# Gates of a gated linear attention computed beside the Fourier products of the same mixer

## The chip, the core and the metric

The kernel is one program on one core of a Trainium2 chip. The metric is the device time of one execution in microseconds (us). The five engines are named as in the profile: PE (TensorE, the matrix products; PEld is its weight load), DVE (VectorE), ACT (ScalarE), POOL (GpSimd) and SP (SyncE, which here only issues transfers).

## What is computed

The reference runs two transformer blocks of two layers each, one after the other. The stage that matters here is the mixer of the first layer of the second block, on 256 context and 512 latent tokens (768 in all). Its input projection gives a part for a Fourier mix, the queries, keys, values and output gate of a gated linear attention (GLA), and a 16-wide `z` from which the decay gates of both directions are made:

```python
def fourier_mix(u):
    ug = u.reshape(B_, L, FOURIER_GROUPS, FOURIER_GROUP_DIM).astype(jnp.float32)
    f = jnp.fft.fft2(ug, axes=(1, 3), norm='ortho').real
    ...
def even_mix(h, s_f, s_b, w_in, w_gate, b_gate, g_gla, w_out):
    p = h @ w_in
    u_f, q, k, v, r, z = jnp.split(p, EVEN_SPLITS, axis=-1)
    loga = [heads(jax.nn.log_sigmoid(zf @ w_gate[d] + b_gate[d]) / GLA_GATE_TEMP, GLA_DK) for d in range(2)]
    o_f, s_f = gla_scan(q, k, v, loga[0], s_f)
    o_b, s_b = gla_scan(flip(q), flip(k), flip(v), flip(loga[1]), s_b)
    ...
    y = jnp.concatenate([fourier_mix(u_f), o], axis=-1) @ w_out
```

`gla_scan` walks over chunks of tokens. Inside a chunk the scores are q·k weighted with the exponential of a difference of the running sums of `loga`, and a state is carried from chunk to chunk. Everything is in float32.

## The kernel before

Activations lie with features on the 128 partitions and tokens along the free axis. Large products run over weight tiles of 128 columns, which SP fetches, ACT and DVE split into a high and a low part (lines 282 and 290), and PE multiplies (lines 312 and 338). Each engine has its own program written out by hand (`pe_program`, `act_program`, `dve_program`, `pool_program`, `sp_program`). An instruction waits only for the semaphores that it names (`seen`), and an engine runs its instructions strictly in the order of its program. So the order of the work around the change is the order of calls in these five functions.

Four stages follow each other in this mixer:

- **Input product** (`pe_in2`, `act_in2`). 17 tiles. Tiles 0 to 8 go to `z2` (keys, queries, output gate, `z`), 9 to 16 to `more` (values in 0 to 3, Fourier input in 4 to 7). At its end PE turns the four value tiles (line 583) into PSUM banks 4 and 5, and ACT copies each out to `v2` (line 592).
- **Fourier** (`pe_fourier`, `act_fourier`, `dve_fourier`). Four groups. For each, PE multiplies with the feature basis `dft_f` into banks 4 to 6 (line 1760), ACT copies the rows to `more[:, 0:2]` (line 1779), and PE multiplies these with the token bases `dft_ctx` and `dft_lat` into banks 4 and 5 (line 1768). ACT copies them out (lines 1783 and 1784) and rounds them to `h_hi` (line 1786), and DVE makes `h_lo` (line 520). One set of buffers serves all groups, so each step waits for the one before.
- **Gates** (`pe_gl_gates`, `act_gl_gates`, `dve_gl_gates`), once per direction: a product with 16 rows (line 1839), copies out with the bias (1849), minus the absolute value on DVE (1863), exponential (1853), a table load (1855), logarithm (1856), then on DVE the log-sigmoid (1865), the running sum with a reset at each chunk (1871), and for the second direction a reversal (1879 and 1881).
- **Scores** (`pe_gla`, `act_gla`, `dve_gla`). Score 0 is the diagonal. Then come 14 steps, 7 levels for each direction. In a step DVE makes the arguments of the decay (lines 634 and 635), ACT the exponential (641), DVE multiplies it with q and k (650), PE makes the products (734) and DVE copies those under a mask into `gatt` (760). Scores 0, 1, 2, 8 and 9 are wide (24 products of 128 columns in three groups), the other ten are narrow (48 rows of the trace, products of 64 columns, in two groups). DVE makes the arguments one step ahead. After these come the state products and the normalization, and then the output product.

The gates of direction 0 are made ahead of score 0, and those of direction 1 between scores 2 and 3. The masks come as 640 KB of int32 into the space of `gatt`. POOL widens them into uint8 masks in 15 casts (line 698) and zeroes `gatt` after that (line 1831). The first masked copy waits for the zeroing.

What runs on both sides of the changed stretch is the product of `in2` on PE and the last products of the scores:

```python
    for i in range(steps):
        c = gl_combs(k)[i % 3]
        pe.wait_ge(*k.seen("decayed", ("g", i)))
        pe_scores(k, "g", i + 1, c, c, GL_UNITS, GL_STEPS)
```

## Time and profile before

| what | us |
|---|---|
| three runs, median (lowest to highest) | 2997.51 (2995.91 to 3006.83) |
| the profiled execution, its own time | 2994.43 |
| its span in the profile | 2993.1 |
| PE, DVE and ACT busy in the span | 2644.7, 1786.8 and 1079.9 |
| window 1441 to 1508 (turning, Fourier): PE busy | 50.45 of 67 |
| window 1508 to 1527 (gates of direction 0): PE and DVE busy | 3.71 and 9.54 of 19 |
| window 1527 to 1554 (scores 0 to 2): PE and DVE busy | 18.18 and 24.00 of 27 |
| window 1554 to 1574 (gates of direction 1): PE and DVE busy | 9.91 and 9.38 of 20 |
| window 1574 to 1640 (scores 3 to 14): PE and DVE busy | 55.23 and 60.48 of 66 |

All times in the trace count from the start of the span. The timeline merges neighbouring instructions of one kind: start, duration, engine, line, operation, tiles, count, and in brackets how long the engine had been idle and who ended that. The chain of waits is the sequence of work that ended last, followed back from the end: what stands in it set the end, and what doesn't was covered. PEclk is the granted clock of PE as a share of 2.4 GHz: 1.00 is that level, 0.50 is 1.2 GHz, and values between are means over a window in which both occurred.

### The profile page before, as it was taken

The page shows a single profiled execution, that of the slowest core. Times are in us where ns is not written, and L with a number is a line of the kernel's source. Part 1 is how long each engine was busy: PE and PEld are TensorE (multiplying, and loading weights), DVE is VectorE, ACT ScalarE, POOL GpSimd, SP SyncE. Part 2 cuts the span into 40 slices and gives each one's busy share as a digit, 9 for nine tenths or more (in the row PEclk, how much of TensorE's full clock was granted, in tenths as well). Part 3 has the DMA queues.
Part 4 walks back from the last instruction along what each step waited for, and adds up shares of the span by engine and source line. Part 5 has one row for each costly group of instructions (what it writes and reads, how often), then busy time and mean ns, then how long its engine had stood idle before and what let it go on. Part 6 is the DMA issues. An engine that isn't in the chain of part 4 may idle for free.

```text
span 2993.1 us, 32376 instructions
## 1 busy us (share of the span) xinstructions
PE 2644.7 (88%) x13240; PEld 2200.5 (74%) x13240; DVE 1786.8 (60%) x2436; ACT 1079.9 (36%) x1413; POOL 32.7 (1%) x48
## 2 busy tenths in 40 slices
PE   5946589999939999989857899999999888899999
PEld 4846377888827888868537778888888766678887
DVE  6574668888688877741059455524553577465464
ACT  3242244323245325342233453312332555343342
...
DMA packets 80275, 295.06 MB, mean 99 GB/s; under 512 B 8944, under 2 KB 11632, under 8 KB 79872
## 3 DMA queue, kind: packets, MB, share of 16 engines
...
## 4 chain that ended last, share of the span: by engine, by line
PE 79%; DVE 13%; ACT 5%; issue 2%; DMA 0%; POOL 0%; DVEq 0%; ACTq 0%
PE ps L312 66%; PE ps L338 3%; PE ps L734 2%; PE ps L2326 1%; PE ps L1768 1%; PE ps L2294 1%; DVE gatt L760 1%; DVE h_lo L520 1%; DVE w_lo L290 1%; DVE p_lo L2596 1%; DVE anm L2578 1%; PE ps L1005 1%; DVE x L1344 1%; ACT h_hi L514 0%; DVE x L1357 0%
## 5 line engine op out<-in xcount | busy, mean ns | idle before, releaser
L312 PE MATMUL ps<-h_hi,w_hi 128*128 128x512 f32 (+1 forms) x2416 | 811.8, 371 | 64.5 <-DVE w_lo L290 38.0
L312 PE MATMUL ps<-h_lo,w_hi 128*128 128x512 f32 (+1 forms) x2416 | 805.0, 368 | 0.0
L312 PE MATMUL ps<-h_hi,w_lo 128*128 128x512 f32 (+1 forms) x2416 | 804.9, 368 | 0.0
L290 DVE TENSOR_TENSOR w_lo<-w_raw,w_hi 128x1024 fp32r<-128x1024 f32 (+2 forms) x323 | 414.7, 1284 | 573.8 <-ACT w_hi L282 573.1
L282 ACT ACTIVATE w_hi<-w_raw 128x1024 fp32r<-128x1024 f32 (+2 forms) x323 | 357.5, 1107 | 876.8 <-PE ps L312 843.4
L312 PEld LDWEIGHTS ps<-h_hi,w_hi 128*128 128x128 f32 x2416 | 456.5, 189 | 150.2 <-DVE w_lo L290 42.2
L312 PEld LDWEIGHTS ps<-h_hi,w_lo 128*128 128x128 f32 x2416 | 456.2, 189 | 77.6
L312 PEld LDWEIGHTS ps<-h_lo,w_hi 128*128 128x128 f32 x2416 | 456.6, 189 | 76.4 <-issue 2.2
L312 PE MATMUL ps<-g_hi,w_hi 128*128 128x512 f32 (+1 forms) x880 | 295.7, 369 | 0.8 <-DVE w_lo L290 0.8
L312 PE MATMUL ps<-g_lo,w_hi 128*128 128x512 f32 (+1 forms) x880 | 294.8, 368 | 0.0
L312 PE MATMUL ps<-g_hi,w_lo 128*128 128x512 f32 (+1 forms) x880 | 294.8, 368 | 0.0
L434 DVE CUSTOM_DVE_ANT_0 m_raw<-m_raw,c_act,small 128x1024 f32<-128x1024 f32 x179 | 226.4, 1280 | 1.6 <-DMA m_raw<-in_ada_w 1.6
L359 DVE SCALAR_TENSOR_TENSOR x<-ps,mods,x 128x512 f32<-128x512 f32 (+1 forms) x112 | 75.3, 690 | 198.0 <-PE ps L312 190.2
L312 PEld LDWEIGHTS ps<-g_hi,w_hi 128*128 128x128 f32 x880 | 165.3, 188 | 29.6 <-DVE w_lo L290 1.4
L312 PEld LDWEIGHTS ps<-g_lo,w_hi 128*128 128x128 f32 x880 | 165.3, 188 | 28.2 <-issue 0.5
L312 PEld LDWEIGHTS ps<-g_hi,w_lo 128*128 128x128 f32 x880 | 165.3, 188 | 27.8
L1487 DVE SCALAR_TENSOR_TENSOR conv_u<-ps,small,conv_u 128x510 f32<-128x510 f32 (+2 forms) x220 | 148.6, 692 | 3.1
L1443 ACT ACTIVATE g_hi<-gated 128x512 fp32r<-128x512 f32 (+1 forms) x88 | 60.4, 686 | 223.8 <-DVE gated L1500 223.8
L1438 ACT ACTIVATE silu_u<-conv_u 128x512 f32<-128x512 f32 (+1 forms) x88 | 60.4, 687 | 191.9 <-DVE conv_u L1487 191.9
L338 PE MATMUL ps<-h_hi,w_hi 128*128 128x256 f32 (+1 forms) x192 | 66.0, 399 | 60.9 <-DVE w_lo L290 35.2
L1502 DVE TENSOR_TENSOR g_lo<-gated,g_hi 128x512 fp32r<-128x512 f32 (+1 forms) x88 | 66.8, 759 | 66.2 <-ACT g_hi L1443 66.2
L338 PEld LDWEIGHTS ps<-h_hi,w_hi 128*128 128x128 f32 x192 | 37.6, 203 | 77.2 <-issue 52.7
...
## 6 DMA issues: line engine op xcount, KB each, us to landing
...
```

Source lines behind the costliest of these rows:

```text
L282: act.activation(k.w_hi[s][:, 0:w], k.w_raw[s][:, 0:w], ACT.Copy).then_inc(*k.tick("w_hi", g))
L290: dve.tensor_tensor(k.w_lo[s][:, 0:w], k.w_raw[s][:, 0:w], k.w_hi[s][:, 0:w].bitcast(F32), ALU.subtract).then_inc(*k.tick("w_lo", g))
L312: last = pe.matmul(ps[:, bank, 0:tn], a[:, c, :], b[:, c, t0:t0 + tn], start=c == 0 and n == 0, stop=c == kt - 1 and n == 2)
L338: last = pe.matmul(ps[:, bank, 0:tn], a, b[:, c, t0:t0 + tn], start=c == 0 and n == 0, stop=c == KD - 1 and n == 2)
L359: last = dve.scalar_tensor_tensor(x, k.ps[:, 2 * s + bank, 0:tn], gates[bank], x, ALU.mult, ALU.add)
L434: dve.tensor_tensor_reduce(w, w, k.c_act[:, last, :], 1.0, bias, ALU.mult, ALU.add, column(last)).then_inc(*k.tick("mods", job.key))
L520: k.nc.vector.tensor_tensor(k.h_lo[:, f, ts], value, k.h_hi[:, f, ts].bitcast(F32), ALU.subtract).then_inc(*k.tick("h_lo", key))
L734: last = pe.matmul(out, lhs[rows, cols], right, start=True, stop=True)
L1438: act.activation(f["silu"][:, :], f["conv"][0][:, :], ACT.Silu).then_inc(*k.tick("silu", g))
L1443: act.activation(f["hi"][:, j, :], f["g"][:, :], ACT.Copy).then_inc(*k.tick("g_hi", (block, layer, half, j)))
L1487: last = dve.scalar_tensor_tensor(o, ps[:, bank, lo - d:hi - d], w, o, ALU.mult, ALU.add)
L1502: dve.tensor_tensor(f["lo"][:, j, :], f["g"][:, :], f["hi"][:, j, :].bitcast(F32), ALU.subtract).then_inc(*k.tick("g_lo", key))
```

## The change

Gates of both directions move into the Fourier stage. The Fourier stage itself gets a second set of row buffers and of PSUM banks (0 to 3 by turns for the token products, 4 to 6 for the features), and its feature products run one group ahead. The turning of the values alternates between two pairs of banks. The running sums go to the upper half of `h_hi`, the log gates to the upper half of `h_lo` (both are free once the input product is done), the reset pattern and the chunk ends to places of their own. The reset pattern is loaded before the input product's later tiles. The masks now land in the space of `gkdt0`, so that POOL zeroes `gatt` first; each cast signals by itself, and each masked copy waits for its own mask. The same signals replace the single one in the HGRN stage of the first block.

```diff
+        self.gtop = Place(nc, sb.at + 4 * 4 * TALL)("gtop", [P, 4 * TALL])
...
+        self.greset = fo("greset", [P, TALL])[:, :]
+        self.gends = fo("gends", [P, 2, 12])
...
-        self.gb = [gl(f"gb{d}", [P, 2 * TALL]) for d in range(2)]
+        self.gb = [self.gtop[:, d * 2 * TALL:(d + 1) * 2 * TALL] for d in range(2)]
...
@@ pool_masks
+        pool.tensor_copy(mask_of(masks, steps, i).rearrange("p (u c) -> p u c", c=n), part.unsqueeze(1).to_broadcast([P, 1 if n == P else 4 * directions, n])
+                         ).then_inc(*k.tick("mask_" + label, i))
@@ dve_scores
+    dve.wait_ge(*k.seen("mask_" + label, i))
@@ sp_in2
+    sp.dma_start(k.greset, k.ins["reset2"]).then_inc(*k.tick("load", "reset2", 16))
@@ pe_fourier
+    pe_gl_gates(k, 0)
+    pe_fo_values(k)
+    pe_fo_features(k, 0)
+    pe_gl_gates(k, 1)
+    for g in range(4):
+        if g + 1 < 4:
+            pe_fo_features(k, g + 1)
+        pe_fo_time(k, g)
...
+def pe_fo_features(k, g):
+    pe = k.nc.tensor
+    if g == 0:
+        pe.wait_ge(*k.seen("load", "dft"))
+        pe.wait_ge(*k.seen("turned_out", ("v2", 3)))
+    else:
+        pe.wait_ge(*k.seen("fourier_rows", g - 1))
...
+def pe_fo_time(k, g):
+    pe, a = k.nc.tensor, fo_rows(k, g)
+    pe.wait_ge(*k.seen("fourier_rows", g))
+    pe.wait_ge(*(k.seen("fourier_out", g - 2) if g >= 2 else k.seen("gl_biased", 1)))
...
+def act_fourier(k):
+    act_gl_biased(k, 0)
+    for f in range(4):
...
+        act.activation(k.v2[:, :, f * P:(f + 1) * P], got, ACT.Copy).then_inc(*k.tick("turned_out", ("v2", f)))
+    act_fo_rows(k, 0)
+    act_gl_biased(k, 1)
+    for d in range(2):
+        act_gl_exp(k, d)
+    act_fo_rows(k, 1)
+    for d in range(2):
+        act_gl_log(k, d)
     for g in range(4):
+        act_fo_out(k, g)
+        if g + 2 < 4:
+            act_fo_rows(k, g + 2)
...
+def dve_fourier(k):
+    dve, q = k.nc.vector, gl_views(k)[0]
+    dve.tensor_scalar(q, q, 0.125, None, ALU.mult).then_inc(*k.tick("gl_q"))
+    for d in range(2):
+        dve_gl_abs(k, d)
+    for d in range(2):
+        dve_gl_gates(k, d)
     for g in range(4):
-        dve_low(k, "fourier", g, slice(0, TALL), k.more[:, 2, :])
+        dve_low(k, "fourier", g, slice(0, TALL), k.rstd[:, :])
@@ sp_gla
-    sp.wait_ge(*k.seen("h_lo", ("fourier", 3)))
-    sp.dma_start(k.greset, k.ins["reset2"]).then_inc(*k.tick("load", "reset2", 16))
     sp.wait_ge(*k.seen("load", "reset2"))
-    sp.dma_start(mask_stage(k.gatt, 2), k.ins["masks2"]).then_inc(*k.tick("load", "masks2", 16))
+    sp.wait_ge(*k.seen("fourier_t", 3))
+    sp.dma_start(mask_stage(k.gkdt[0], 2), k.ins["masks2"]).then_inc(*k.tick("load", "masks2", 16))
@@ pool_gla
+    pool.wait_ge(*k.seen("fourier_t", 3))
+    pool.memset(k.gatt[:, :, :], 0.0).then_inc(*k.tick("zeroed", "g"))
     pool.wait_ge(*k.seen("load", "masks2"))
-    pool_masks(k, "g", k.gmasks, k.gatt, 2)
-    pool.wait_ge(*k.seen("masks", "g"))
-    pool.memset(k.gatt[:, :, :], 0.0).then_inc(*k.tick("zeroed", "g"))
+    pool_masks(k, "g", k.gmasks, k.gkdt[0], 2)
@@ pe_gla
-    pe.wait_ge(*k.seen("h_lo", ("fourier", 3)))
-    pe_gl_gates(k, 0)
     pe.wait_ge(*k.seen("gl_k2"))
...
-        if i + 1 == 2:
-            pe.wait_ge(*k.seen("kept", BASE["in2"] + 16))
-            pe_gl_gates(k, 1)
-            pe.wait_ge(*k.seen("gl_biased", 1))
@@ act_gla
-    act_gl_gates(k, 0)
     for i in range(len(GL_STEPS)):
         act_decay(k, "g", i, gl_combs(k)[i % 3], s16)
-        if i == 2:
-            act_gl_gates(k, 1)
@@ dve_gla
-    dve.tensor_scalar(q, q, 0.125, None, ALU.mult).then_inc(*k.tick("gl_q"))
-    dve_gl_gates(k, 0)
+    dve.wait_ge(*k.seen("fourier_t", 3))
     dve.tensor_scalar(comb, kk, 2.0, None, ALU.mult).then_inc(*k.tick("gl_k2"))
...
-        if i == 2:
-            dve_gl_gates(k, 1)
```

PE in the Fourier stage, from the feature product of group 0 on. Of before (1760 are features, 1768 token products):

```order
L1760 MATMUL ps<-dft_f,z2more 128x256 [waits turned_out,load]
L1760 MATMUL ps<-dft_f,z2more 128x256 x5
L1768 MATMUL ps<-dft_ctx,z2more 128x256 [waits fourier_rows]
L1768 MATMUL ps<-dft_ctx,z2more 128x256 x3
L1768 MATMUL ps<-dft_lat,z2more 128x512 x8
L1760 MATMUL ps<-dft_f,z2more 128x256 [waits fourier_out]
L1760 MATMUL ps<-dft_f,z2more 128x256 x5
L1768 MATMUL ps<-dft_ctx,z2more 128x256 [waits fourier_rows]
L1768 MATMUL ps<-dft_ctx,z2more 128x256 x3
```

Of the change (1785 features, 1906 gates, 1798 token products):

```order
L1785 MATMUL ps<-dft_f,z2more 128x256 [waits turned_out,load]
L1785 MATMUL ps<-dft_f,z2more 128x256 x5
L1906 MATMUL ps<-z_143,tmp_68 128x256 [waits gl_biased]
L1906 MATMUL ps<-z_143,tmp_68 128x512
L1906 MATMUL ps<-z_143,tmp_68 128x256
L1906 MATMUL ps<-z_143,tmp_68 128x512
L1785 MATMUL ps<-dft_f,z2more 128x256 [waits fourier_rows]
L1785 MATMUL ps<-dft_f,z2more 128x256 x5
L1798 MATMUL ps<-dft_ctx,z2more 128x256 [waits gl_biased,fourier_rows]
L1798 MATMUL ps<-dft_ctx,z2more 128x256 x3
L1798 MATMUL ps<-dft_lat,z2more 128x512 x8
```

The gate products of direction 1 and the features of group 1 now stand ahead of the token products of group 0, and no feature product waits for `fourier_out` any more.

DVE from the end of the Fourier stage to the first arguments of the decay. Of before (520 is `h_lo` of the four groups, 2088 the doubled keys that score 0 needs):

```order
L520 TENSOR_TENSOR h_lo<-z2more,h_hi 128x768 [waits h_hi] x4
L2086 TENSOR_SCALAR z_142<-z_142 128x1536
L1863 SCALAR_TENSOR_TENSOR gb_147<-gcomb 128x1536 [waits gl_biased]
L1865 SCALAR_TENSOR_TENSOR gcomb<-gcomb,gb_147 128x1536 [waits gl_log]
L1871 SCALAR_TENSOR_TENSOR gb_147<-spare,gcomb 128x768 [waits load,gl_loga]
L1871 SCALAR_TENSOR_TENSOR gb_147<-spare,gcomb 128x768
L1875 COPY gends<-gb_147 128x12 [waits gl_b]
L2088 TENSOR_SCALAR gcomb<-z_142 128x1536
L634 TENSOR_TENSOR gkdt_152<-gb_147 128x768 [waits gl_q]
L635 TENSOR_TENSOR gkdt_152<-gb_147 128x768
L634 TENSOR_TENSOR spare<-gb_147 128x384x2
```

Of the change (1842 scales q, 1937 to 1958 are the gates of both directions, 521 is `h_lo`):

```order
L1842 TENSOR_SCALAR z_143<-z_143 128x1536
L1937 SCALAR_TENSOR_TENSOR gtop<-spare 128x1536 [waits gl_biased] x2
L1944 SCALAR_TENSOR_TENSOR spare<-spare,gtop 128x1536 [waits gl_log]
L1950 SCALAR_TENSOR_TENSOR gtop<-greset,spare 128x768 [waits load,gl_loga]
L1950 SCALAR_TENSOR_TENSOR gtop<-greset,spare 128x768
L1954 COPY gends<-gtop 128x12 [waits gl_b]
L1944 SCALAR_TENSOR_TENSOR spare<-spare,gtop 128x1536 [waits gl_log]
L1950 SCALAR_TENSOR_TENSOR gtop<-greset,spare 128x768 [waits gl_loga]
L1950 SCALAR_TENSOR_TENSOR gtop<-greset,spare 128x768
L1956 TENSOR_TENSOR gtop<-gtop,spare 128x1536 [waits gl_b]
L1958 TENSOR_TENSOR gends<-gtop,spare 128x12 [waits gl_back]
L521 TENSOR_TENSOR h_lo<-rstd,h_hi 128x768 [waits h_hi] x4
```

The whole gate work stands ahead of the four `h_lo` operations, and the doubled keys follow straight behind these.

DVE between the masked copies of score 2 and those of score 3. Of before:

```order
L760 COPY_PREDICATED gatt<-gmasks,ps 128x2x512 [waits scored] x2
L1863 SCALAR_TENSOR_TENSOR gb_148<-gkdt_151 128x1536 [waits gl_biased]
L1865 SCALAR_TENSOR_TENSOR gkdt_151<-gkdt_151,gb_148 128x1536 [waits gl_log]
L1871 SCALAR_TENSOR_TENSOR gb_148<-spare,gkdt_151 128x768 [waits gl_loga]
L1871 SCALAR_TENSOR_TENSOR gb_148<-spare,gkdt_151 128x768
L1879 TENSOR_TENSOR gb_148<-gb_148,gkdt_151 128x1536 [waits gl_b]
L1881 TENSOR_TENSOR gends<-gb_148,gkdt_151 128x12 [waits gl_back]
L634 TENSOR_TENSOR spare<-gb_147 128x48x16 [waits scored,gl_back]
L635 TENSOR_TENSOR spare<-gb_147 128x48x16
L650 TENSOR_TENSOR gkdt_152<-gkdt_152,z_142 128x96x8 [waits decay]
L650 TENSOR_TENSOR gkdt_152<-gkdt_152,z_142 128x96x8
```

Of the change:

```order
L762 COPY_PREDICATED gatt<-gmasks,ps 128x2x512 [waits scored] x2
L635 TENSOR_TENSOR spare<-gtop 128x48x16 [waits scored]
L636 TENSOR_TENSOR spare<-gtop 128x48x16
L651 TENSOR_TENSOR gkdt_153<-gkdt_153,z_143 128x96x8 [waits decay]
L651 TENSOR_TENSOR gkdt_153<-gkdt_153,z_143 128x96x8
L762 COPY_PREDICATED gatt<-gmasks,ps 128x128x4 [waits scored,att,mask_g]
```

The six operations of the second direction's gates are gone from between them, and the masked copy has one more name among its waits.

## Rows read from the trace of the kernel before

**Rows 1.** Page: shares of the chain that ended last, by engine.
```profile
PE 79%; DVE 13%; ACT 5%; issue 2%; DMA 0%; POOL 0%; DVEq 0%; ACTq 0%
```

**Rows 2.** Chain of waits, Fourier stage: start us, us, engine, tile, line.
```profile
1442.16 0.89 PE ps L583 x6
...
1448.58 0.82 ACT v L592
1449.53 2.84 PE ps L1760 x12
...
1463.72 2.87 PE ps L1760 x12
...
1468.12 8.87 PE ps L1768 x24
...
1477.94 2.87 PE ps L1760 x12
```

**Rows 3.** Chain of waits, from the last Fourier product to the first scores.
```profile
1499.84 5.59 PE ps L1768 x13
...
1507.23 0.97 DVE h_lo L520
...
1508.34 3.72 PE ps L1839 x8
...
1512.08 2.00 ACT gcomb L1849 x4
...
1526.65 0.86 DVE gcomb L2088
```

**Rows 4.** Timeline of DVE around the gates of the second direction.
```profile
1553.16 1.29 DVE L760 COPY_PREDICATED gatt<-gmasks,ps 128x1024 f32<-128x1024 uint8 x1 [1.01 <-PE ps L734]
...
1573.94 0.96 DVE L634 TENSOR_TENSOR spare<-gb 128x768 f32<-128x768 f32 x1
...
1575.68 1.82 DVE L650 TENSOR_TENSOR gkdt<-gkdt,z 128x768 f32<-128x768 f32 x2
1577.42 1.83 DVE L760 COPY_PREDICATED gatt<-gmasks,ps 128x512 f32<-128x512 uint8 x2
```

**Rows 5.** Timeline of PE: Fourier products, gate products, groups of scores.
```profile
1455.73 7.03 PE L1768 MATMUL ps<-dft_lat,z2more 128*128 128x512 f32 x16
...
1553.04 5.48 PE L1839 MATMUL ps<-z,tmp 16*128 16x256 f32 x8
...
1604.87 2.08 PE L734 MATMUL ps<-spare 64*128 64x128 f32 x16 [0.77 <-DVE gatt L760]
...
1612.98 1.16 PE L734 MATMUL ps<-gcomb 64*128 64x128 f32 x16 [0.77 <-DVE gatt L760]
1613.98 2.79 PE L734 MATMUL ps<-gkdt 64*128 64x64 f32 x48
```

**Rows 6.** Chain of waits, the last three steps of scores.
```profile
1624.20 15.73 PE ps L734 x144
```

**Rows 7.** Timeline of POOL, and two operations of DVE beside it.
```profile
1516.49 12.78 POOL L698 CAST gmasks<-gatt 128x128 uint8<-128x128 int32 x15 [657.12 <-DMA gatt<-in_masks]
1529.32 2.66 POOL L1831 MEMSET gatt<- 128x3072 f32 x1
...
1528.71 1.36 DVE L635 TENSOR_TENSOR gkdt<-gb 128x768 f32<-128x768 f32 x1
1529.99 0.95 DVE L634 TENSOR_TENSOR spare<-gb 128x768 f32<-128x768 f32 x1
```

**Rows 8.** Windows of 5 us: busy us of PE, PEld, DVE, ACT, POOL, then PEclk.
```profile
1505.00:1510.00 5.00, 2.08 (x7) 1.11 (x7) 1.83 (x2) 1.71 (x3) 0.00 (x0) 1.00 0.16 34
1510.00:1515.00 5.00, 2.05 (x4) 0.43 (x2) 0.89 (x1) 1.99 (x4) 0.00 (x0) 0.51 0.35 111
...
1590.00:1595.00 5.00, 5.00 (x50) 5.00 (x48) 5.00 (x7) 1.48 (x1) 0.00 (x0) 0.50 0.01 3
```

**Rows 9.** DMA issues: KB each, us from issue to landing.
```profile
gatt<-in_masks SPq DMA_DIRECT2D x1, 640.0 KB, 3.8
```

122 lines of the change are left out of this document (63 added, 59 removed).

## The prediction

> **What bounds the kernel now.** I read the views from the outside in. The page's chain by engine says that PE's products end 79% of the span [rows 1], so anything off PE pays only where PE stands still. The windows by stage (the table above) show where that is: in the gates of direction 0 PE works 3.7 us of 19, in those of direction 1 9.9 of 20. The chain of waits then tells what ends each stretch. In the Fourier stage it alternates between PE and ACT: features 2.87 us, the copy of the rows, token products 8.87 us, the copy out, and from one group's features to the next's 1477.94 - 1463.72 = 14.22 us [rows 2]. PE works 11.74 of these and waits 2.48. Behind the last token product the chain runs through one engine after another, none busy beside the other: `h_lo`, the gate products, the biased copies, then on to the doubled keys [rows 3]. The same happens for direction 1 between scores 2 and 3 [rows 4]. From score 3 on DVE and PE are both full, and the last three steps belong to PE [rows 6].
>
> **The change, part by part.** Times are on the clock of the old trace, where the last product tile has been copied at 1442.1.
>
> *1. The Fourier stage.* PE now makes the gate products of direction 0 first. Their 4 products are 2 of 256 and 2 of 512 columns; a 512-column product is two rows of 7.03/16 = 0.44 us [rows 5], so at that clock 4 x 0.44 + 4 x 0.22 = 2.7 us, to about 1444.9. Measured nearby are 3.72 (where the clock falls in the middle, [rows 3]) and 5.48 us at half clock [rows 5], which are the upper bounds; I take 2.7, since PE comes from a dense product at full clock. ACT's biased copies take 2.00 us [rows 3], then four copies of turned values at 0.82 [rows 2]: 1444.9 + 2.0 + 3.3 and some handing over, 1450.9. PE turns tiles 2 and 3 in that time. Features 0 start there, 1.4 us later than before [rows 2], and the values' two pairs of banks save what the gates would otherwise have cost. Then PE does 4 features (2.87 each), the second gate products (2.7) and 4 token products (8.87 each): 49.7 us, to about 1500.5, against 1499.84 + 5.59 = 1505.4 before [rows 3]. **Gain 4.9 us.** Nothing of it waits, if ACT keeps up: rows 0 end at 1455.5, the biased copies of direction 1 at 1458.5, and the token products of group 0 start at 1459.3; this is the tightest place, with 0.8 us. The two exponentials, rows 1, the table load and the two logarithms are done by about 1467.8, when those products end at 1468.2. DVE's gate work follows at 1466: two log-sigmoids of 1.8, four sums of 1.7 to 2.0, a reversal of 1.8, in all to about 1479.5. The copy out of group 1 waits for `h_lo` of group 0 behind that, about 1480.5, and PE needs that buffer and rows 3 only at 1491, 7 us later. So the gates cost nothing on the path but their two products.
>
> *2. From the last token product to score 0.* Before: from 1505.4 to the doubled keys at 1526.65 [rows 3], 21.2 us. Now: copies out, `h_hi`, `h_lo`, which end at 1508.20 [rows 3], 2.8 us after the products, and the doubled keys follow at once, since they stand behind `h_lo` of group 3 on DVE's queue. **Gain 18.4 us.** Beside it stand POOL's zeroing (2.66 us [rows 7], done at 1503.2) and the masks: 3.8 us from issue to landing [rows 9], 1504.3, and the first cast is a short one. The first masked copy comes at about 1511. None of the two is late, and the casts, 12.8 us for 15 [rows 7], keep ahead of steps of 5 to 8 us. ACT's table load stands behind the last `h_hi` and ends before the first argument does.
>
> *3. Between scores 2 and 3.* Before: from 1553.16 + 1.29 = 1554.45 to the arguments at 1573.94, 19.5 us [rows 4]; all of it goes. What is late next is PE: the 48 products of score 3 may start only when score 2 has been copied, and take 15.73/3 = 5.24 us at half clock [rows 6]. DVE needs 1577.42 - 1573.94 = 3.5 us to the masked copies and 0.9 for their first half, so the second half waits 0.9 us or a little more. From there both engines go at 5.2 us a step and the lag stays. **Gain 19.5 - 1.1 = 18.4 us.**
>
> *4. POOL beside DVE.* The casts used to run beside the sums and the first arguments, now beside the first two pairs of arguments, the first products with q and k and the first masked copies. The trace shows one operation at 1.36 us beside the casts and its like at 0.95 without [rows 7]. Four operations of DVE more than before are exposed: 4 x 0.41 = 1.7 us. Bounds: 0 if the casts slip between, 4 us if the three masked copies and the second step's operations suffer as well. **Loss 1.7 us.** The Trainium skill (GPSIMD Engine Reference, 1. Specifications) says that POOL shares its SBUF interfaces with VectorE and contends with instructions that have two SBUF inputs; a masked copy here reads its data from PSUM, so by that rule it stays clear and the loss ends at these 1.7 us. The row on the arguments agrees with it.
>
> *5. The rest.* The 384 KB of the reset pattern now queue behind the Fourier bases, ahead of a weight tile. I count nothing for it; the tile is due one whole product after its issue. 15 masked copies in this stage wait for one signal more; a copy with two satisfied waits starts while its predecessor ends (1575.68 + 1.82 = 1577.50 against 1577.42 [rows 4]), so I count 0, and at most 0.1 us each, 1.5 us. The HGRN stage keeps its order: 0.
>
> **Sum.** 4.9 + 18.4 + 18.4 - 1.7 = 40.0 us off the profiled execution's 2994.43, which gives 2954.4. The runs shown have their median 3.1 us above that execution; against it the forecast is 2997.5 - 40 = **2957.5 us**.
>
> **The rivals.**
>
> *The clock stays up.* After the Fourier stage the granted clock was 1.00, then 0.51 as PE did the 16-row gate products and stopped [rows 8]. This gap shrinks to 3.7 us, and the one between scores 2 and 3 vanishes. If PE kept 2.4 GHz through the scores, a wide group would take 1.16 in place of 2.08 us and a narrow score 2.79 in place of 5.24 [rows 5, 6]: five wide scores save 0.9 each, the lag of 1.1 us goes, and the end, where PE alone is the chain, becomes bound by DVE, about 4.5 us less. In all 10 us, 2947 us. Against it: from 1590 to 1595 PE was busy 5.00 of 5.00 us and its clock was 0.50 [rows 8], so being busy with these half-height products did not raise it. The Trainium skill (TensorE: Matmul & The Clock Gate, What's actually happening) has it that activity of PE releases the throttled clock; taken as PE's busy time, that speaks for this rival, and the row speaks against it. Chance 8%.
>
> *The Fourier stage doesn't close up.* ACT's queue is now long, and strictly in order: if a logarithm or a biased copy is late, token products wait as before. At worst all four gaps of 2.48 us stay, and PE still has 5.4 us of gate products more: the gain of 4.9 turns into a loss of 5. Result 2967 us. The slack of 0.8 us in part 1 speaks for a part of it, the 7 us behind it against more. Chance 10%.
>
> *The gates cool the clock, and the change loses.* The two gate products use 16 of 128 rows, and the clock fell during such products at 1510 [rows 8]. If they now pull the clock down at 1443 and again at 1454, and it doesn't come back, the 47 us of features and token products take twice the time: 47 + 5 us more against a gain of 40, so 3009 us, 0.4% slower than before; it decides from 40 us of PE's work at half clock. Against it: the old stage turned values with PE idle half of the time and kept 1.00. And the full-height products come in blocks of over 8 us, after which I expect it back. A short dip costs 3 to 5 us, and is in the range. Chance 2%.
>
> *The waits are there anyway.* Something I take as covered (landing of the masks, zeroing, a table load) takes the place of the gates' chain in part 2. The most that could stand there is the masks' landing and all 15 casts, which would hold the masked copy of score 0 to 1517, 6 us late: 2963 us. The casts signal one by one, so this means that the change doesn't do what it says. Chance 4%.
>
> **How the numbers follow.** The forecast with its small terms has 76%, the rivals 8, 10, 2 and 4%. The likeliest case with its bounds (casts 0 to 4 us, waits up to 1.5, a dip of the clock up to 5, and some us that a median of runs moves) goes from 2950 to 2966. The range reaches to the clock rival and to the Fourier rival: **2945 to 2968**. A measurement of this kernel can tell about 0.5%, 15 us, from no change. Faster by more than that: all cases but the slower one and mishaps of over 25 us that I can't name, 95%; within: 4%; slower by more: 1%.
>
> **What would show it.** In the changed profile: the token products of the groups with no idle time of PE between groups; the last one ending near 1500.5; the doubled keys about 2.8 us behind; POOL's casts from about 1504; no idle stretch of DVE between scores 2 and 3 but about 1 us; the clock at 0.5 in the scores again. The forecast is wrong if PE waits at the token products, if the clock stands below 1.00 after 1450, or if the masked copy of score 0 waits for a mask.

## The result, and the profile after

The change took **2956.47 us** (median of 4 runs, 2951.5 to 2959.81) beside 2996.71 us before (median of 4): a ratio of 0.9861, with a 95% interval from 0.9829 to 0.9894, or 40.2 us less. The forecast was 2957.5 us, in a range of 2945 to 2968. The profiled execution of the change took 2959.81 us, its span is 2958.5.

To see where the time went, the trace is cut at four points that every kernel here has: the first product behind the input product's last tile (start), the end of the last token product, the first masked copy, and the end of the last one. Behind these the work runs on to the first product of the output projection, which closes the **stretch**.

| | before | after | forecast |
|---|---|---|---|
| start to end of the last token product | 63.26 | 59.55 | 58.3 |
| from there to the doubled keys | 21.14 | 2.69 | 2.8 |
| from there to the first masked copy | 28.05 | 9.88 | |
| first to last masked copy | 107.77 | 88.12 | |
| last masked copy to the output projection | 37.79 | 37.97 | |
| the stretch (sum without the second row) | 236.87 | 195.52 | 196.9 |
| ahead of the start | 1442.2 | 1434.8 | |
| behind the stretch | 1314.1 | 1328.2 | |

The stretch is 41.3 us shorter, the forecast 40.0. Outside it the change only moves the loading of the reset pattern and splits the masks' signal in the first block, and there the one execution is 7 us shorter ahead and 14 longer behind. That is told under the control run below; it is the reason why the stretch, and not the span, is compared from here on.

One execution of `control` took 4478.48 us at a mean granted clock of 0.554, and the ratios below leave it out.

The page's chain now has PE at 80% (79% before, [rows 1]) and DVE at 12%:

```profile
PE 80%; DVE 12%; ACT 4%; issue 2%; DMA 0%; POOL 0%; DVEq 0%; ACTq 0%
```

The timeline of PE in the Fourier stage answers to [rows 2]. 1906 is the gate products, 1772 the turning, 1785 features, 1798 token products; the bracket is the idle time before:

```profile
1434.83 3.32 PE L1906 MATMUL ps<-z,tmp 16*128 16x256 f32 x8 [1.05 <-ACT z2more L351]
1438.08 5.68 PE L1772 MATMUL ps<-ident,z2more 128*128 128x128 f32 x24
1444.75 2.83 PE L1785 MATMUL ps<-dft_f,z2more 128*128 128x256 f32 x12 [0.99 <-ACT v L1809]
1447.51 2.84 PE L1906 MATMUL ps<-z,tmp 16*128 16x256 f32 x8
1450.28 4.54 PE L1785 MATMUL ps<-dft_f,z2more 128*128 128x256 f32 x12
...
1463.26 2.75 PE L1785 MATMUL ps<-dft_f,z2more 128*128 128x256 f32 x12
...
1474.44 2.75 PE L1785 MATMUL ps<-dft_f,z2more 128*128 128x256 f32 x12
```

Behind 1444.75 no row of this view has a bracket until the last token product ends: PE never waits again in this stage. A group takes 1474.44 - 1463.26 = 11.18 us, where it took 14.22. One row stands out: the features of group 1 took 4.54 us, their likes 2.75. The windows (busy us of PE, PEld, DVE, ACT, POOL, then PEclk) show what went with it. Up to the last token product three windows have a granted clock below 1.00, and each holds gate products or what stands right behind them:

```profile
1435.00:1440.00 5.00, 5.00 (x17) 3.13 (x17) 0.00 (x0) 1.81 (x4) 0.00 (x0) 0.70 0.01 3
1440.00:1445.00 5.00, 3.97 (x18) 3.20 (x17) 1.76 (x1) 3.31 (x5) 0.00 (x0) 0.62 0.00 0
...
1450.00:1455.00 5.00, 5.00 (x15) 3.88 (x15) 1.76 (x1) 4.16 (x6) 0.00 (x0) 0.66 0.00 0
```

The gate work on DVE, in its timeline, ends at 1472.20 + 0.18, and `h_lo` of group 0 follows:

```profile
1472.20 0.18 DVE L1958 TENSOR_TENSOR gends<-gtop,spare 128x12 f32<-128x12 f32 x1
1472.30 0.95 DVE L521 TENSOR_TENSOR h_lo<-rstd,h_hi 128x768 fp32r<-128x768 f32 x1
```

The chain of waits behind the last token product answers to [rows 3]. The gate products, the biased copies and the logarithm are gone from it:

```profile
1477.19 17.20 PE ps L1798 x48
...
1496.19 0.96 DVE h_lo L521
1497.15 0.87 DVE gcomb L2153
```

DVE goes on from there to score 3 nearly without a break; the timeline near the start and at the end of that answers to [rows 4]. 635 and 636 are the arguments, 651 the decayed products, 762 the masked copies:

```profile
1498.81 1.04 DVE L636 TENSOR_TENSOR gkdt<-gtop 128x768 f32<-128x768 f32 x1
...
1501.70 2.64 DVE L651 TENSOR_TENSOR gkdt<-gkdt,z 128x768 f32<-128x768 f32 x2
1504.26 2.48 DVE L762 COPY_PREDICATED gatt<-gmasks,ps 128x1024 f32<-128x1024 uint8 x2
...
1523.18 1.29 DVE L762 COPY_PREDICATED gatt<-gmasks,ps 128x1024 f32<-128x1024 uint8 x1 [1.00 <-PE ps L735]
1524.37 0.94 DVE L635 TENSOR_TENSOR spare<-gtop 128x768 f32<-128x768 f32 x1
...
1530.04 1.25 DVE L762 COPY_PREDICATED gatt<-gmasks,ps 128x1024 f32<-128x1024 uint8 x1 [1.51 <-PE ps L735]
```

The arguments follow the copies of score 2 at once (1524.37), where 19.5 us lay between them. What is late next is PE, as its own timeline (the row that answers to [rows 5] and [rows 6]) shows: 5.38 us for the 48 products of score 3, at a granted clock of 0.50 (window 1525 to 1530), and DVE's last row above waits 1.51 us for them.

```profile
1524.62 5.38 PE L735 MATMUL ps<-gcomb 64*128 64x64 f32 x48 [1.48 <-DVE gatt L762]
```

POOL zeroes first and casts behind it (compare [rows 7]); the masks land ahead of the first cast:

```profile
1494.44 2.66 POOL L1885 MEMSET gatt<- 128x3072 f32 x1 [639.58 <-PE ps L1798]
1498.33 10.86 POOL L699 CAST gmasks<-gkdt 128x128 uint8<-128x128 int32 x15 [1.24 <-DMA gkdt<-in_masks]
```

The narrow scores keep their clock of [rows 8], 0.50 with PE busy 5.00 of 5.00 us. In windows with wide scores it is above 0.50 at times, as it was before.

```profile
1530.00:1535.00 5.00, 5.00 (x51) 5.00 (x50) 4.96 (x6) 1.48 (x1) 0.00 (x0) 0.50 0.01 3
```

### The profile page after: what moved, and what is told of

It is laid out like the page before. It is cut to its first block, busy times and chain, and to the rows that moved or that the text cites. A ratio compares the mean times of both kernels' runs of the same rounds, so it can differ in the third digit from the quotient of the medians.

```text
span 2958.5 us, 32375 instructions
## 1 busy us (share of the span) xinstructions
PE 2654.1 (90%) x13240; PEld 2208.0 (75%) x13240; DVE 1786.1 (60%) x2436; ACT 1076.8 (36%) x1411; POOL 30.7 (1%) x48
## 4 chain that ended last, share of the span: by engine, by line
PE 80%; DVE 12%; ACT 4%; issue 2%; DMA 0%; POOL 0%; DVEq 0%; ACTq 0%
PE ps L313 67%; PE ps L339 3%; PE ps L735 2%; PE ps L2389 1%; PE ps L1798 1%; PE ps L2357 1%; DVE gatt L762 1%; DVE h_lo L521 1%; DVE w_lo L291 1%; DVE p_lo L2659 1%; DVE anm L2641 1%; DVE x L1346 1%; DVE x L1359 0%; ACT h_hi L515 0%; PE ps L1007 0%
```

## The experiments

Eleven further runs were made, in three groups, each with the kernel before on the same chip. The stretch and its parts, from one profiled execution of each:

| kernel | Fourier | to the first masked copy | masked copies | rest | stretch | ratio to before [95%] |
|---|---|---|---|---|---|---|
| before | 63.26 | 28.05 | 107.77 | 37.79 | 236.87 | |
| the change | 59.55 | 9.88 | 88.12 | 37.97 | 195.52 | 0.9861 [0.9829, 0.9894] |
| control | 56.44 | 9.88 | 88.10 | 38.17 | 192.59 | 0.9859 [0.9812, 0.9906] |
| again | 56.48 | 9.88 | 88.09 | 38.20 | 192.65 | 0.9846 [0.9823, 0.9868] |
| gates0_back | 53.97 | 27.63 | 87.72 | 40.01 | 209.33 | 0.9916 [0.9882, 0.995] |
| gates1_back | 55.32 | 9.88 | 106.93 | 37.93 | 210.06 | 0.9904 [0.9877, 0.9931] |
| serial_fourier | 69.40 | 9.88 | 88.10 | 38.25 | 205.63 | 0.9889 [0.9859, 0.9919] |
| masks_once | 56.61 | 17.56 | 88.84 | 39.63 | 202.64 | 0.9893 [0.9876, 0.9909] |
| early_masks | 59.56 | 8.78 | 89.16 | 37.98 | 195.48 | 0.9864 [0.9849, 0.9879] |
| tall_gates | 55.72 | 9.88 | 88.12 | 39.60 | 193.32 | 0.9868 [0.9842, 0.9894] |
| filler | 56.43 | 9.89 | 110.53 | 39.81 | 216.66 | 0.9931 [0.9916, 0.9947] |
| early0 | 59.48 | 1.78 | 88.83 | 38.89 | 188.98 | 0.982 [0.9796, 0.9844] |
| early0_tall | 55.72 | 1.79 | 89.72 | 37.64 | 184.87 | 0.9808 [0.9785, 0.9832] |

The last part (the column "rest") moves by itself by up to 2.4 us. In `gates0_back`, `masks_once`, `tall_gates`, `filler` and `early0` the last four products before the output projection took 2.66 to 2.90 us, in the other traces 1.53, and all but the last of these five also took longer over the first products with `v`. The work there is the same in all, and `tall_gates`, whose edit is far ahead of it, has 39.60 us where `control` has 38.17.

### The change itself, twice more

Neither has an edit.

> The changed kernel once more, to see what moves between two executions of one program. My theory: the stretch from the end of the input product to the first product of the output projection is fixed by its queues and repeats to 1 us (194.6 us in the trace of the change, 236.9 in that of before), and what the total moved less than that (34.6 us between the two spans, not 42.3) belongs to the other stages: dense weight products there take 8.32 us a tile in some stretches and 8.48 in others, the same in both kernels but in other places. Rival: the change itself puts the slower pace into the feed-forward stage behind it; then this run shows 8.48 us there again, and 8.32 in the input product.

> The change once more, unchanged, beside the two kernels below on one chip. The times outside the changed stretch differed by some 14 us between the profiled executions so far, with ACT's split of a 1024-row weight tile coming every 8.32 us in some stretches and every 8.48 in others. Theory (this is a property of the execution and not of the kernel): a median within 2952 to 2962 us and a stretch of 192.6 to 195.5 us, and some stretches of weight products at 8.32 and some at 8.48 us again. Rival (the first profiled run of the change was the odd one): all stretches at 8.32 us and a span near 2947 us.

Measured: stretches of 192.59 and 192.65 us, so 44.2 us below before; the first trace of the change, at 195.52, had 3 us more, all of it in the Fourier stage. So the theory of `control` that the stretch repeats to 1 us fails, between the first trace and the two repeats. (Its 194.6 us for that trace end one block of products early, at 1629.38; to the landmark of the table it is 195.52.) The median of `again` was 2953.49 us beside 2996.21. In the parts outside the stretch, the first trace of the change has 1328.2 us behind it, control 1317.2. Where these differ can be seen on ACT, which splits a weight tile of 1024 rows each time PE has finished one. In the input product, two stretches of the same work, of before and of the change, each at a granted clock of 1.00. Before:

```profile
1356.50 1.06 ACT L282 ACTIVATE w_hi<-w_raw 128x1024 fp32r<-128x1024 f32 x1 [6.66 <-PE ps L312]
...
1364.98 1.06 ACT L282 ACTIVATE w_hi<-w_raw 128x1024 fp32r<-128x1024 f32 x1 [6.66 <-PE ps L312]
```

The change:

```profile
1359.00 1.06 ACT L283 ACTIVATE w_hi<-w_raw 128x1024 fp32r<-128x1024 f32 x1 [6.50 <-PE ps L313]
...
1367.32 1.06 ACT L283 ACTIVATE w_hi<-w_raw 128x1024 fp32r<-128x1024 f32 x1 [6.50 <-PE ps L313]
```

A tile comes every 8.48 us in the one and every 8.32 in the other. Both paces occur in both kernels: behind the stretch, before goes at 8.32 and the first trace of the change, from 1738 on, at 8.48, and `control` and `again` go at 8.48 ahead and 8.32 behind. Of the twelve traces with the change or a part of it, four (the first one, gates0_back, serial_fourier, tall_gates) go at 8.48 over most of what lies behind the stretch and take 1327 to 1329 us there, the other eight go at 8.32 and take 1317 to 1318. Ahead of it, the six traces with 8.48 start the stretch at 1437.6 to 1443.4, and before, which goes at 8.48 there too, at 1442.2: the work on the first block and the moved loading show no price. So it is the theory of `again` that holds: 11 of the 14 us behind the stretch belong to the execution and not to the change. The other 3 are in all twelve traces, against one trace of before; aligned with it, those of control arise in the attention, 650 to 890 us behind the stretch. Why, was not looked into; if they belong to the change, it is worth 44.2 - 3 = 41 us in all.

### Each direction's gates put back

gates0_back: direction 0 as before, behind the Fourier stage.

```diff
@@ pe_fourier
-    pe_gl_gates(k, 0)
@@ act_fourier
-    act_gl_biased(k, 0)
...
-    for d in range(2):
-        act_gl_exp(k, d)
+    act_gl_exp(k, 1)
...
-    for d in range(2):
-        act_gl_log(k, d)
+    act_gl_log(k, 1)
@@ dve_fourier
-    for d in range(2):
-        dve_gl_abs(k, d)
-    for d in range(2):
-        dve_gl_gates(k, d)
+    dve_gl_abs(k, 1)
+    dve_gl_gates(k, 1)
@@ pe_gla
+    pe_gl_gates(k, 0)
     pe.wait_ge(*k.seen("gl_k2"))
@@ act_gla
+    act_gl_biased(k, 0)
+    act_gl_exp(k, 0)
+    act_gl_log(k, 0)
@@ dve_gla
+    dve_gl_abs(k, 0)
+    dve_gl_gates(k, 0)
```

> The changed kernel with the gates of direction 0 made behind the Fourier stage again, those of direction 1 beside it. Theory (each part pays by itself, as predicted): the doubled keys come about 21 us behind the last token product in place of 2.8, while the Fourier stage gets shorter by one gate product and its biased copies, 3 us; the stretch becomes 194.6 + 18.4 - 3 = about 210 us, the ratio to before about 0.991. Rival (the two directions share one cover, so that taking one back costs less): below 203 us.

Measured: 209.33 us, 16.7 above control; 1.8 of these are in the rest, which moves by itself. The chain of waits has back what [rows 3] showed, the gate products, the biased copies and, 18.7 us behind the products' start, the doubled keys:

```profile
1499.51 4.66 PE ps L1900 x8
...
1504.19 2.01 ACT spare L1909 x4
...
1518.22 0.87 DVE gcomb L2151
```

The first masked copy comes 27.63 - 9.88 = 17.75 us later, and the Fourier stage is 2.5 us shorter without one set of gate products, although its features of group 1 took 4.54 us here.

gates1_back: direction 1 as before, between scores 2 and 3. The edit in the Fourier stage mirrors the one above; in the scores:

```diff
@@ pe_gla
+        if i + 1 == 2:
+            pe_gl_gates(k, 1)
+            pe.wait_ge(*k.seen("gl_biased", 1))
@@ act_gla
+        if i == 2:
+            act_gl_biased(k, 1)
+            act_gl_exp(k, 1)
+            act_gl_log(k, 1)
@@ dve_gla
+        if i == 2:
+            dve_gl_abs(k, 1)
+            dve_gl_gates(k, 1)
```

> The changed kernel with the gates of direction 1 between scores 2 and 3 again. Theory: 19.5 us come back there, less 1.1 us of PE's lag in score 3, and the Fourier stage gets shorter by the second gate product and the cold features behind it, 3 to 4 us; the stretch becomes about 209 to 210 us, the ratio about 0.991. Rival (the clock, which is at half in both cases, rises in the gap's place and gives part of it back): 203 us or less.

Measured: 210.06 us, 17.5 above control. In DVE's timeline the gap of [rows 4] is back: score 2's copies end at 1524.91 + 3.84 = 1528.75 and the arguments come at 1547.26, 18.5 us later. The masked copies take 106.93 us in place of 88.10, and the Fourier stage is 1.1 us shorter: the gate products are gone, and PE waits 1.54 us for the rows of group 0, which they used to cover.

```profile
1524.91 3.84 DVE L762 COPY_PREDICATED gatt<-gmasks,ps 128x1024 f32<-128x1024 uint8 x3
...
1547.26 0.95 DVE L635 TENSOR_TENSOR spare<-gtop 128x768 f32<-128x768 f32 x1
```

The parts add up. Undone one at a time, direction 0 gives back 17.75 us up to the first masked copy, where the whole change took away 28.05 - 9.88 = 18.17, and direction 1 gives back 18.83 between the masked copies, where it took away 107.77 - 88.10 = 19.67. With the Fourier stage's 63.26 - 56.44 = 6.82 us, 17.75 + 18.83 + 6.82 = 43.4, and the whole change has 44.3 in control.

### The Fourier groups one after the other

```diff
@@ pe_fourier
-        if g + 1 < 4:
-            pe_fo_features(k, g + 1)
+        if g:
+            pe_fo_features(k, g)
@@ pe_fo_features
-        pe.wait_ge(*k.seen("fourier_rows", g - 1))
+        pe.wait_ge(*k.seen("fourier_out", g - 1))
@@ act_fourier
-    act_fo_rows(k, 1)
...
-        if g + 2 < 4:
-            act_fo_rows(k, g + 2)
+        if g + 1 < 4:
+            act_fo_rows(k, g + 1)
```

> The changed kernel with the gates beside the Fourier stage, but each group's features only after the copy out of the group before, as in the old one. Theory: three gaps of 2.48 us come back, +7.4 us, the stretch becomes 202 us, ratio 0.988. Rival (the gates' work on ACT delays the rows when there is no group of lead, so that more than the gaps comes back): +10 us or more. Rival in the other direction (the lead is worth nothing): +2 us or less.

Measured: 205.63 us, 13.0 above control, all in the Fourier stage (69.40 against 56.44). PE's timeline:

```profile
1456.55 3.44 PE L1798 MATMUL ps<-dft_ctx,z2more 128*128 128x256 f32 x8 [2.18 <-ACT spare L1914]
...
1467.81 2.86 PE L1785 MATMUL ps<-dft_f,z2more 128*128 128x256 f32 x12 [0.96 <-ACT rstd L1834]
1472.21 1.99 PE L1798 MATMUL ps<-dft_ctx,z2more 128*128 128x256 f32 x8 [1.54 <-ACT z2more L1825]
...
1482.03 2.86 PE L1785 MATMUL ps<-dft_f,z2more 128*128 128x256 f32 x12 [0.96 <-ACT rstd L1834]
```

A group is back at 1482.03 - 1467.81 = 14.22 us, 3.04 more than in the change; three times that is 9.1. The first wait, 2.18 us, is for the biased copies of direction 1: the features of group 1 no longer cover them. And 3.44 in place of 1.89 us goes with a dip of the clock (0.66 in the window from 1455 to 1460). Together 9.1 + 2.2 + 1.6 = 12.9. Feature products a group ahead thus cover ACT's copies and also part of the gates. The forecast of this run had the three waits and missed the other two terms; the first rival's number, 10 us or more, is what came, though PE waited for the biased copies and not for the rows.

### The masks in one go

```diff
@@ pool_gla
-    pool.wait_ge(*k.seen("fourier_t", 3))
-    pool.memset(k.gatt[:, :, :], 0.0).then_inc(*k.tick("zeroed", "g"))
     pool.wait_ge(*k.seen("load", "masks2"))
     pool_masks(k, "g", k.gmasks, k.gkdt[0], 2)
+    pool.wait_ge(*k.seen("mask_g", 2 * LEVELS))
+    pool.memset(k.gatt[:, :, :], 0.0).then_inc(*k.tick("zeroed", "g"))
```

> Undoes only the making of the masks step by step: POOL casts all 24 masks first and zeroes gatt after them, so that the one signal that the first masked copy waits for comes last again. In the trace of the change the casts begin about 1.3 us after the doubled keys start and take 15 x 0.72 us, the zeroing 2.66 us. Theory (this part is worth a term of its own, hidden in the 28.05 to 9.88 us that the first masked copy moved ahead): with all 24 casts and the zeroing in a row, the first masked copy starts 16 to 19 us after the last token product in place of 9.88, and the stretch from the Fourier stage to the output projection grows by 6 to 9 us over the repeat of the change (192.6 us), to 199 to 202 us; the product of score 1 waits with it. Rival (masks don't matter, the gates did it all): the first masked copy stays within 1 us of 9.88 and the stretch within 1 us of 192.6.

Measured: the first masked copy 17.56 us behind the last token product, and the stretch at 202.64, 10.0 above control. In DVE's timeline it waits 7.60 us, and for POOL:

```profile
1511.74 2.47 DVE L762 COPY_PREDICATED gatt<-gmasks,ps 128x1024 f32<-128x1024 uint8 x2 [7.60 <-POOL gatt L1887]
```

7.7 us of the 10.0 are this wait. Of the other 2.3, some 0.7 stand between the masked copies, where I did not follow them up, and 1.5 in the rest, which moves by itself. That is also why the stretch lies above the 199 to 202 us expected. With the gates gone from in front of the scores, POOL's casts and its zeroing would have been what comes last. Masks step by step are worth 7.7 us beside the other two parts. By themselves they would have been worth nothing, by the trace of before (no run has them alone): there POOL was done at 1529.32 + 2.66 = 1531.98 [rows 7], and the first masked copy came 1.5 us later, right behind DVE's own work:

```profile
1533.47 2.47 DVE L760 COPY_PREDICATED gatt<-gmasks,ps 128x1024 f32<-128x1024 uint8 x2
```

### The casts ahead of the scores

```diff
+        self.gmasks = Place(nc, sb.at + 4 * (KD + 6) * TALL)("gmasks", [P, mask_columns(2)], U8)
@@ sp_gla
-    sp.wait_ge(*k.seen("fourier_t", 3))
+    sp.wait_ge(*k.seen("fourier_f", 3))
@@ pool_gla
-    pool.wait_ge(*k.seen("fourier_t", 3))
-    pool.memset(k.gatt[:, :, :], 0.0).then_inc(*k.tick("zeroed", "g"))
     pool.wait_ge(*k.seen("load", "masks2"))
+    pool.wait_ge(*k.seen("gl_back", 1))
     pool_masks(k, "g", k.gmasks, k.gkdt[0], 2)
+    pool.wait_ge(*k.seen("fourier_t", 3))
+    pool.memset(k.gatt[:, :, :], 0.0).then_inc(*k.tick("zeroed", "g"))
```

> Moves the masks' transfer and their casts on POOL ahead, into the Fourier stage (the byte masks lie in other space, so that they need not wait for the last token product); only the zeroing of gatt stays where it was. No POOL cast is then beside the DVE work of steps 0 to 2. Theory (the part 4 of the prediction: casts on POOL slow DVE's operations from SBUF): the decay arguments beside them fall from 1.04 and 0.95 to about 0.87 us, the two decayed products of step 0 from 2.64 to about 1.8, and the stretch by 0.8 to 1.6 us, from 192.6 to 191 to 191.8. Rival (no contention, the long operations are long for another reason): the same durations and the same stretch. Second risk: casts beside DVE's biased copies in the Fourier stage lengthen that by up to 1 us.

Measured, on DVE's timeline (the decayed products of step 0) and on POOL's:

```profile
1502.29 1.82 DVE L651 TENSOR_TENSOR gkdt<-gkdt,z 128x768 f32<-128x768 f32 x2
```

```profile
1482.01 6.82 POOL L699 CAST gmasks<-gkdt 128x128 uint8<-128x128 int32 x15 [626.20 <-DMA gkdt<-in_masks]
```

The contention is real, and works both ways: the two decayed products take 1.82 us where they took 2.64, the casts 6.82 in place of 10.86. It is worth 9.88 - 8.78 = 1.1 us up to the first masked copy. But the last masked copy came no earlier: 8.78 + 89.16 = 97.94 us behind the last token product, control 97.98. The gain is still there at score 3 (its products start 28.34 us behind the last token product, control 29.32), and goes in scores 9 and 10, where PE worked at half clock here and at the full one in control: the last group of score 9 took 2.08 us against 1.16, the next 48 products 5.22 against 2.79. So the price is confirmed at 1.1 us up to the first masked copy, while the expected gain of the stretch, 0.8 to 1.6 us, did not come: it is 195.48 us, with the clock's dip in a Fourier stage of 59.56, and would be 192.4 with the stage of control, 56.44.

### Gate products over all 128 rows

```diff
-    wg = k.tmp[0][0:16, :].rearrange("p (f c) -> p f c", c=P)
+    wg = k.tmp[0][:, :].rearrange("p (f c) -> p f c", c=P)
...
-            last = pe.matmul(..., wg[:, 2 * d + f, :], k.z2[0:16, 8, t0:t0 + tn], ...)
+            last = pe.matmul(..., wg[:, 2 * d + f, :], k.z2[:, 8, t0:t0 + tn], ...)
```

> The gate products contract over all 128 rows of z's ninth tile and of the gate weights in place of the 16 that hold something (the others are zero, so the sums are the same). Theory (the dip of the granted clock in the Fourier stage to 0.62 to 0.70, and with it the features of group 1 at 4.54 us and turning at 5.68 us in the trace of the change, comes from the products of only 16 rows, which the throttle counts as little work): the granted clock stays at 1.00 from the start of the Fourier stage to its end, features of group 1 take 2.8 us and turning 4.7 us, and the Fourier stage takes 55 to 56 us (change 59.6, its repeat 56.4). Rival (the dip comes from something else in the stage, say waits): the clock falls again to 0.6 to 0.7 somewhere in the first 25 us, and the stage stays at 56 to 60 us.

Measured: the granted clock is 1.00 in every window from 1425 to 1500, the stage takes 55.72 us, and `early0_tall` below repeats that figure. PE's timeline:

```profile
1443.37 2.82 PE L1906 MATMUL ps<-z,tmp 128*128 128x256 f32 x8 [1.05 <-ACT z2more L351]
...
1454.21 2.74 PE L1906 MATMUL ps<-z,tmp 128*128 128x256 f32 x8
1456.79 2.75 PE L1785 MATMUL ps<-dft_f,z2more 128*128 128x256 f32 x12
```

The products cost the same (2.82 against 2.81 us in control), and the features of group 1 take 2.75 us. With 16 rows all ten traces show a dip, the seven with the stage as the change has it among them, and in these it takes 56.4 to 56.6 us in four and 59.5 in three. That speaks for the 16-row products as the cause of the dips; two traces with 128 rows, both without one, are what it rests on. Waits of PE are not what the dip goes with: this trace has one of 1.48 us in the turning and kept 1.00. The gain is 0.7 to 3.8 us of the Fourier stage, too little for the ratio (0.9868) to show; the stretch, 193.32 us, has 1.4 us more in the rest.

### Filling PE's waits in the scores

```diff
+def pe_warm(k, bank, n):
+    for _ in range(n):
+        k.nc.tensor.matmul(k.ps[:, bank, 256:512], k.h_hi[:, 0, 0:P], k.h_hi[:, 0, 0:256], start=True, stop=True)
...
@@ pe_gla
+    pe_warm(k, 4, 24)
     pe.wait_ge(*k.seen("gl_k2"))
...
+        if is_wide(GL_STEPS, j):
...
+            pe_warm(k, 0, 12)
+        else:
...
+            pe_warm(k, 4 if j % 2 else 0, 8)
```

> Fills PE's waits in the scores with products of full height that nobody reads (24 ahead of score 0, 12 before wide steps, 8 before narrow ones), each some 0.11 us at the full clock and 0.21 at half. Theory (rival 1 of the prediction turned into a test: the scores run at a granted clock of 0.5 because their own products have half height and PE idles between them, and this sets their time): the clock goes to 0.8 to 1.00 in the scores, their narrow steps fall from 5.2 to about 3.5 to 4 us each, and the stretch falls by 5 to 10 us to 183 to 188. Rival A (the clock stays at 0.5 whatever stands in the waits): 8 products of 0.21 us are in each narrow step's chain, the stretch grows by up to 8 x 1.7 = 14 us. Rival B (the clock rises but the steps are set by DVE's masked copies and ACT): the narrow steps stay above 5 us and the stretch within 2 us of 192.6.

Measured: the masked copies take 110.53 us, 22.4 more, so rival A holds, and more than it said. PE's timeline, and one of the windows (PEclk is the third number from the end):

```profile
1577.98 2.08 PE L1965 MATMUL ps<-h_hi 128*128 128x256 f32 x8 [1.39 <-DVE gatt L762]
1579.99 5.39 PE L735 MATMUL ps<-gkdt 64*128 64x64 f32 x48
...
1587.31 3.04 PE L735 MATMUL ps<-spare 64*128 64x64 f32 x26
```

```profile
1585.00:1590.00 5.00, 5.00 (x38) 4.66 (x36) 4.58 (x5) 1.49 (x1) 0.00 (x0) 0.50 0.00 0
```

A narrow step takes 1587.31 - 1579.99 = 7.32 us in place of 5.2, since the 8 fillers stand in PE's own chain at half clock, 2.08 us. Ten narrow steps make 21 us of the 22.4. In the narrow scores products of full height did not bring the clock back.

In the wide scores they came with a clock of 1.00, and against control it was worth nothing. There the filler window

```profile
1515.00:1520.00 5.00, 4.77 (x60) 4.32 (x60) 4.92 (x6) 0.67 (x1) 0.00 (x0) 1.00 0.00 0
```

has 1.00 (0.66 in control), and the first 32 products of scores 1 and 2 took 2.06 us each (3.64 and 3.39 in control). Yet from the first masked copy to the arguments behind score 2 it took 19.2 us in both. The last group of each of these two scores took 1.16 us in control already, and with that DVE sets the time, as rival B had it. Nor does the full clock shorten a narrow score while DVE works beside it. In control score 10 ran at it, 2.79 us, and PE then waited 2.22 us for DVE, whose own work is 5.2 us a step:

```profile
1564.72 2.79 PE L735 MATMUL ps<-gkdt 64*128 64x64 f32 x48
1569.73 5.01 PE L735 MATMUL ps<-spare 64*128 64x64 f32 x48 [2.22 <-DVE spare L651]
```

So a narrow score costs PE at 1.2 GHz as much as it costs DVE. Among the narrow scores PE alone sets the time only at score 3, where DVE waits 1.51 us, and in the last three [rows 6].

### Step 0 made ahead

The masks as in early_masks, and in the Fourier stage also the doubled keys, the arguments, the exponential and the decayed products of step 0, which are taken out of their old places. The diff shows the main lines.

```diff
@@ act_fourier, in the loop over groups
+        if g == 1:
+            act_decay(k, "g", 0, step_comb(k, 0), 1.0 / 16.0)
@@ dve_fourier
-    for g in range(4):
+    for g in range(2):
         dve_low(k, "fourier", g, slice(0, TALL), k.rstd[:, :])
...
+    dve_decay_arg(k, "g", 0, e0, step_comb(k, 0), 0, False)
...
+    dve_decayed(k, "g", 0, step_comb(k, 0), 0, False, q, kk)
...
+    dve.tensor_scalar(comb, kk, 2.0, None, ALU.mult).then_inc(*k.tick("gl_k2"))
+    dve_low(k, "fourier", 2, slice(0, TALL), k.rstd[:, :])
...
+def step_comb(k, i):
+    turned, upper, comb = gl_combs(k)
+    return (upper, turned, comb)[i % 3]
@@ pool_gla
+    pool.memset(k.gatt[:, 12:24, :], 0.0)
...
+    pool.memset(k.gatt[:, 0:12, :], 0.0).then_inc(*k.tick("zeroed", "g"))
@@ dve_gla, behind the copies of score 0
+        if i == 0:
+            dve_low(k, "fourier", 3, slice(0, TALL), k.rstd[:, :])
```

> Takes what the other runs showed one step on: the masks' transfer and casts, the doubled keys and the decay arguments and decayed products of step 0 are made in the Fourier stage, in DVE's and POOL's idle time (the three places for decayed keys swap roles, so that step 0's lie where nothing else is then), the low half of features of group 3 follows score 0's masked copies, and gatt is zeroed in two halves. Between the last token product and the first masked copy stood the doubled keys (0.95), four arguments (4.07) and two decayed products (2.64), of which only score 0's own products (3.1 us on PE) and half of the zeroing stay. Theory (the chain behind the last token product is DVE's work of steps 0 to 2, and steps 3 on are bound by PE at half clock, 5.12 us a step, from wherever step 3 starts): the first masked copy comes 3 to 5 us after the last token product in place of 9.88, step 3 starts 5 to 9 us earlier, and the stretch falls to 184 to 188 us from 192.6. Rival (PE sets steps 1 and 2 as well once DVE has less to do, as early_masks gained 1.1 us ahead and gave all of it back by step 3): the stretch falls by 2 us or less.

> The kernel early0 with the gate products over all 128 rows, as in tall_gates, where the granted clock stayed at 1.00 through the Fourier stage and the stage took 55.7 us. Theory (the two gains add, since one is PE's clock in the Fourier stage and the other DVE's work behind it): the Fourier stage within 55 to 56.5 us, the stretch 1 to 4 us below that of early0, and a median 6 to 12 us below that of the change on the same chip. Rival (DVE's added work in the Fourier stage now delays the biased copies or low halves that PE waits for): the Fourier stage grows to 58 us or more.

Measured: `early0` has 188.98 us with the dip in its Fourier stage (59.48), above the 184 to 188 expected; `early0_tall` has 184.87 without the dip. PE's timeline of `early0_tall` around the seam:

```profile
1483.67 7.03 PE L1798 MATMUL ps<-dft_lat,z2more 128*128 128x512 f32 x16
1490.63 2.06 PE L735 MATMUL ps<-z,gcomb 64*128 64x128 f32 x32
...
1512.62 5.38 PE L735 MATMUL ps<-gcomb 64*128 64x64 f32 x48 [1.48 <-DVE gatt L762]
```

Score 0 follows the last token product with no wait at all, and its first 32 rows take 2.06 us, 3.10 in control. Score 3 starts 21.92 us behind it, 29.32 in control: 7.4 us earlier. The masked copies come 1.8 us behind the product, earlier than the 3 to 5 I had expected. The stretch is 192.65 - 184.87 = 7.8 us below that of `again`, and the medians are 2946.23 and **2938.95 us** beside 2953.49 of the change on the same chip (14.5 us less, where 6 to 12 were expected; the times outside the stretch move by as much), so `early0_tall` beats both kernels: 0.9808 [0.9785, 0.9832] of before, an interval that lies below the one of the change in the same session, 0.9846 [0.9823, 0.9868], but for its last 0.001.

## Why the prediction was right

**The sum.** It had 40.0 us; the stretch gave 41.3 in the first trace and 44.2 in the two repeats, and the medians 40.2, and 42.7 in the group of `again`. That the medians agree to a tenth is luck: paces of 8.32 and 8.48 us outside the stretch move an execution by 10 us and more. The mechanism, part by part, is what was forecast; the sizes of parts 1, 3 and 4 were each off by 1 to 2 us.

**1. The Fourier stage, forecast 4.9 us.** Measured 3.7 in the first trace, 6.8 in `control`, whose clock dipped less. Two errors of opposite sign. The sum took each block with its old row, 2.87 and 8.87 us [rows 2]; seamless ones take 2.59 and 8.59 (11.18 a group), 0.28 less for each of seven blocks, 2.0 in all. It is the difference between the 2.48 us of wait that I read and the 3.04 that a group saved. Against that stands the dip, which I had named (3 to 5 us) and kept out of the sum: 3.1 us in the first trace, 9.92 against 8.50 from the first gate product to the features, and 4.54 against 2.86 for the features of group 1. The old trace could not tell that this would be a matter of the execution: 56.4 to 56.6 in some, 59.5 in others. The place with 0.8 us of slack held in every trace but `serial_fourier`, which took its cover away and paid 2.2; in control 0.6 us were left of it. DVE's gate work was to end at 1479.5 on the clock of the old trace; it ended at 1472.38 + 7.33 = 1479.7.

**2. Behind the last token product, forecast 18.4 us.** Measured 21.14 - 2.69 = 18.45 to the doubled keys, 18.2 to the first masked copy, and 17.75 in `gates0_back`.

**3. Between scores 2 and 3, forecast 18.4 us.** The masked copies are 107.77 - 88.12 = 19.65 us shorter, `gates1_back` gives 18.8 for the part alone. PE's lag at score 3 was put at 0.9 us "or a little more", 1.1 in the sum, and is 1.51. What came on top is the clock: the last groups of scores 1 and 8 took 1.16 us in the first trace and 2.08 before, which the sum had left to the first rival.

**4. POOL beside DVE, forecast a loss of 1.7 us.** The rows are there: arguments at 1.04, decayed products at 2.64 for two, and `early_masks` prices all of it at 1.1 us. Against before it is a loss of only 0.3 us, since before had casts beside its own first two arguments, 1.36 us each [rows 7]: from the doubled keys to the first masked copy it took 28.05 - 21.14 = 6.91 us before and 9.88 - 2.69 = 7.19 after. So this term of the sum was mis-sized, 1.7 us for 0.3: it took the price from the row and forgot that the old kernel paid most of it already. By the Trainium skill (GPSIMD Engine Reference, 1. Specifications) instructions with two inputs from SBUF contend with POOL. The trace agrees: arguments (1.04 against 0.95) and decayed products are slowed, and the first masked copies, which read their data from PSUM, take 2.48 us for two beside the casts and 2.47 without.

**5. The rest, forecast 0.** The narrow masked copies with their extra wait take 1.83 us for two, as in [rows 4].

**The rivals.** *The clock stays up* fell: 0.50 in the narrow scores again, and fillers of full height did not lift it there. It came true in a small part, in groups of wide scores, as said under part 3. The Trainium skill (TensorE: Matmul & The Clock Gate, What's actually happening), taken as busy time, would have the clock rise; the narrow scores' window above, with fillers in it, has PE busy 5.00 of 5.00 us and a clock of 0.50. *The Fourier stage doesn't close up*: no wait of PE is left. *The gates cool the clock*: it happened in part, 3 us and not 47, since the clock came back to 1.00 each time, with full-height products running. One sign that the prediction named for being wrong did appear, a clock below 1.00 after 1450: 0.66 in the window from 1450 to 1455 of the first trace, which is 1457 on the old trace's clock. It cost the features of group 1 their 1.7 us and left the rest of the stage at 1.00. *The waits are there anyway* didn't come true because the masks signal one by one; `masks_once` gives 7.7 us of wait where the rival had put 6.
